# Delta rule steps in another order, and who makes the low weight parts of the second block

## The chip, the cores and the metric

The kernel runs on one core of one Trainium2 chip. The metric is the device time of one execution in microseconds (us). TensorE is PE in the profile, VectorE DVE, ScalarE ACT, GpSimd POOL and SyncE SP; SP issues the weight transfers.

## The reference

A sequence of 256 tokens with 1024 channels goes through a first block and then a second block, each of two layers. The change is in the second block, of which this is the mixer between two feed-forward networks, cut to what matters:

```python
hcat = x @ w_in
qa, ka, va, qkv_b, beta_raw, dt_raw, z, gate_raw = jnp.split(hcat, SPLIT_POINTS, axis=-1)
ya = sliding_window_attention(qa, ka, va, pos_bias, sink) @ w_branch_a      # 16 heads
qkv_b = jax.nn.silu(causal_depthwise_conv_2(qkv_b, conv_w))                 # 4 taps
qb, kb, vb = jnp.split(qkv_b, (QK_B, 2 * QK_B), axis=-1)                    # 8 heads of 128
qb, kb = l2norm(qb), l2norm(kb)
beta = jax.nn.sigmoid(beta_raw)
g = -jnp.exp(a_log) * jax.nn.softplus(dt_raw + dt_bias)
o = gated_delta_rule(qb, kb, vb, g, beta)
o = o * lax.rsqrt(jnp.mean(o * o, -1, keepdims=True) + NORM_EPS) * dn_norm_g * jax.nn.silu(z)
gate_a, gate_b = jnp.split(jax.nn.sigmoid(gate_raw), 2, axis=-1)
return (gate_a * ya + gate_b * (o @ w_branch_b)) @ w_out
```

The delta rule is, for each head, S_t = a_t (S_{t-1} - beta_t k_t k_t^T S_{t-1}) + beta_t k_t v_t^T and o_t = S_t^T q_t; the kernel computes it in two chunks of 128 tokens.

## The kernel before

**Weights in two parts.** All weights arrive as float32 in units of 128x2048, through a ring of four slots, issued by SP as slots come free. ACT makes the high part of each unit (L1506, called by split_high) and another engine the low part, weight minus high part (split_low: L1830 on DVE, L901 on GpSimd). PE multiplies three times: high by high, high by low, low by high. So one product round is three matmuls of 256 columns, and most units are 16 rounds, 48 matmuls. Which engine makes a low part is set by close(): GpSimd for the kinds named in by_pool, here "w" (projections) and "gy" (gates), except behind FFN units; DVE for the rest and for the whole first block. Splits are issued in quarters between the steps.

**A plan per block.** plan_second() writes one list of steps. Each engine walks that list in order and does its own part of every step, so the list fixes the order on PE, ACT, DVE and GpSimd at once; semaphores only add waits. A PSUM bank is passed on by two counters, full (PE has written it) and taken (ACT or DVE has read it).

**Weaving.** interleave(chain, dense) puts a chain of small dependent steps between rounds of big products. Each chain step has a weight; behind it as many rounds of the dense units follow as its share of the total weight. When a unit is complete, its follow-up steps come one at a time behind the next chain steps: for a convolution unit the taps of its two halves (DVE L2191, L2193, then tanh on ACT L1731) and silu (DVE L2206).

**The mixer.** First the attention: for head n score (PE L1212; DVE L2011 to L2018; exponentials on ACT L1617 to L1622), turn (transposes, PE L1227), value (PE L1256). cumg (PE L1356, DVE L2159 to L2166, two exponentials on ACT) makes the cumulative decays and stands ahead of score 0. Dense units in this weave are two queries, the convolutions of head pair 0, two z projections (pz) and the convolutions of pair 1.

Then the delta rule, two heads at a time. A head is prepared by five steps: dtr (PE transposes q, k and v, L1371; ACT squares L1745; GpSimd's root L858, L860), dte (six DVE scalars L2216 to L2221, then six scaled copies on DVE L2227 and five on ACT), ddc (PE L1397, DVE L2236, ACT L1776, GpSimd L949), dtf (PE L1383, L1387; DVE L2244), dkk (PE L1406; DVE L2252, L2257). ddc and dkk use bank 3, dtr and dtf banks 6 and 7 (4 and 5 for head 1). dtr waits for the silu of its pair; CO holds one pair's convolutions, so the first taps of the next wait for the second dtr of the pair.

solve() runs a pair a, b: dl0 (PE L1415, DVE L2265, L2267), then six levels of dla a, dla b, dlb a, dlb b. dla is two products (PE L1426) that ACT copies (L1506); dlb is four (PE L1436, L1438) with which DVE updates the inverse (L2274, L2279). Then du1 (L1447), du2 (L1454), du3 (L1460), evacuated by ACT, and du4 (L1468): ACT squares the output (L1796), GpSimd takes the root, DVE waits for the root and scales (L2287). dot transposes the result (PE L1477) and DVE multiplies and splits it (L2294, L1837, L1839). The preparation of the next two heads is inserted in the chain of a pair. Dense units: gate 0 and the convolutions of pair 2 in pair 0; gate 1 and the convolutions of pair 3 in pair 1; two pz and two gates in pair 2; four gates in pair 3. Behind the last pair come the gates of the second branch (gy, PE L1316 and L1322; DVE L2094, L2099) with the output product wo (L1080).

## Time and profile before

| what | us |
| --- | --- |
| median of three runs (lowest, highest) | 3360.16 (3359.53, 3362.44) |
| the profiled execution | 3359.86 |
| its span, first to last instruction | 3358.1 |
| PE busy in the span | 3068.3 |
| DVE busy | 1926.3 |
| ACT busy | 1340.5 |
| GpSimd busy | 526.1 |

Times inside the span count from its first instruction. The second block runs from about 1545 us; its first mixer from 1764 to 2232, its second from 2657 to 3130. Matmul ends are modelled by the profile, so the rate at which PE works is best read from the distance between starts. "idle before" names what ended an engine's idle time; a wait put down to "issue" was for nothing that the profile shows.

### The profile page before, as it was taken

Reading aid. Unit: us, or ns where it says so; the run is one execution under the profiler, and the core shown is the slowest. Engines: PE = TensorE matmul, PEld = TensorE weight load, DVE = VectorE, ACT = ScalarE, POOL = GpSimd, SP = SyncE. Lnnn points to the kernel's source line nnn. Section 1 sums busy time; section 2 is a strip of 40 time slices with the busy share of each in tenths; the row PEclk is TensorE's granted clock in tenths of the full one; section 3 lists DMA queues with packets and bytes.
Section 4 is the critical chain, followed back from the end, with each engine's and each line's share of the span. In section 5 each row is a group of like instructions: output and inputs, shape, how many; then the busy total and the mean of one; then the engine's idle time right before and its main releaser. Section 6 shows DMA issues by size and latency. Waiting matters only on the chain.

```text
span 3358.1 us, 59079 instructions
## 1 busy us (share of the span) xinstructions
PE 3068.3 (91%) x22178; PEld 2902.8 (86%) x22178; DVE 1926.3 (57%) x3302; ACT 1340.5 (40%) x2222; POOL 526.1 (16%) x469
## 2 busy tenths in 40 slices
PE   7999999998999999997998888989989898889897
PEld 7989898997989898996987888879979788789797
DVE  4556776554556776554553666375565536655654
ACT  3344454334344454332334544333333354343332
POOL 1000000000000000000004444430020235345101
PEclk9999999999999999998997999989989899999899
DMA  5544444554544445557552211345545422124453
GB/s 198 186 160 151 132 142 167 186 187 147 187 160 161 130 141 183 173 181 168 203 195 76 101 62 65 114 155 187 189 154 194 143 90 89 66 72 146 159 185 116
DMA packets 72121, 495.48 MB, mean 148 GB/s; under 512 B 8000, under 2 KB 8176, under 8 KB 19856
## 3 DMA queue, kind: packets, MB, share of 16 engines
q1 hardware_dynamic: 67504, 471.95, 41.2%
q0 software_dynamic: 4048, 18.59, 2.1%
q8 instruction: 184, 3.01, 0.4%
q14 instruction: 113, 0.93, 0.1%
q10 hardware_dynamic: 272, 0.99, 0.1%
HBM read 487.31 MB, written 4.19 MB: 146 GB/s over the span
## 4 chain that ended last, share of the span: by engine, by line
issue 75%; PE 11%; DVE 6%; POOL 4%; DVEq 1%; POOLq 1%; ACT 1%; DMA 0%; ACTq 0%; SPq 0%
PE psum L1102 4%; POOL weights_low L901 2%; DVE work L2193 1%; PE psum L1316 1%; POOL small L860 1%; PE psum L1322 1%; PE psum L1212 1%; POOLq L859 0%; DVE normed_t_low L1839 0%; DVE small L2218 0%; DVE work L2279 0%; PE psum L1158 0%; PE psum L1426 0%; DVEq L2196 0%; DVE normed_t_high L1837 0%
## 5 line engine op out<-in xcount | busy, mean ns | idle before, releaser
L1830 DVE TENSOR_TENSOR weights_low<-weight_ring,weights_high 128x2048 fp32r<-128x2048 f32 (+6 forms) x532 | 890.0, 1679 | 796.7 <-ACT weights_high L1506 795.5
L1506 ACT ACTIVATE weights_high<-weight_ring 128x2048 fp32r<-128x2048 f32 (+3 forms) x788 | 906.9, 1171 | 1099.1 <-DMA weight_ring<-stream 1091.1
L1027 PE MATMUL psum<-normed_t_high,weights_high 128*128 128x256 f32 x2816 | 803.5, 285 | 24.8 <-DVE normed_t_low L1839 22.3
L1027 PE MATMUL psum<-normed_t_low,weights_high 128*128 128x256 f32 x2816 | 800.8, 284 | 0.0
L1027 PE MATMUL psum<-normed_t_high,weights_low 128*128 128x256 f32 x2816 | 800.5, 284 | 0.0
L1027 PEld LDWEIGHTS psum<-normed_t_high,weights_high 128*128 128x128 f32 x2816 | 543.8, 193 | 31.5 <-DVE normed_t_low L1839 24.5
L1027 PEld LDWEIGHTS psum<-normed_t_low,weights_high 128*128 128x128 f32 x2816 | 544.6, 193 | 3.6
L1027 PEld LDWEIGHTS psum<-normed_t_high,weights_low 128*128 128x128 f32 x2816 | 544.3, 193 | 0.0
L1080 PE MATMUL psum<-weights_high,work_parts 128*128 128x512 f32 x1664 | 524.3, 396 | 13.9 <-DVE work_parts L1839 13.9
L1102 PE MATMUL psum<-normed_t_high,weights_high 128*128 128x256 f32 x1248 | 395.6, 317 | 11.5 <-DVE normed_t_low L1839 10.5
L901 POOL TENSOR_TENSOR weights_low<-weight_ring,weights_high 128x512 fp32r<-128x512 f32 (+1 forms) x216 | 348.4, 1628 | 307.4 <-ACT weights_high L1506 307.3
L1080 PEld LDWEIGHTS psum<-weights_high,work_parts 128*128 128x128 f32 x1664 | 306.2, 188 | 80.1 <-DVE work_parts L1839 14.4
L1102 PE MATMUL psum<-normed_t_low,weights_high 128*128 128x256 f32 x1248 | 362.2, 290 | 0.0
L1102 PE MATMUL psum<-normed_t_high,weights_low 128*128 128x256 f32 x1248 | 362.0, 290 | 0.0
L858 POOL TENSOR_TENSOR small<-small 128x1 f32<-128x1 f32 (+3 forms) x74 | 17.0, 230 | 2124.5 <-ACT work L1554 974.9
L1080 PE MATMUL psum<-weights_low,work_parts 128*128 128x512 f32 x832 | 328.5, 395 | 0.0
L1102 PEld LDWEIGHTS psum<-normed_t_high,weights_high 128*128 128x128 f32 x1248 | 249.0, 200 | 25.6 <-DVE normed_t_low L1839 11.9
L1102 PEld LDWEIGHTS psum<-normed_t_low,weights_high 128*128 128x128 f32 x1248 | 249.5, 200 | 1.0
L1316 PE MATMUL psum<-normed_t_high,weights_high 128*128 128x256 f32 x768 | 236.7, 308 | 14.8 <-DVE weights_low L1830 9.5
L1102 PEld LDWEIGHTS psum<-normed_t_high,weights_low 128*128 128x128 f32 x1248 | 248.0, 199 | 0.0
L1316 PE MATMUL psum<-normed_t_low,weights_high 128*128 128x256 f32 x768 | 222.7, 290 | 0.0
L1316 PE MATMUL psum<-normed_t_high,weights_low 128*128 128x256 f32 x768 | 222.5, 290 | 0.0
(258 smaller groups left out, 4326.8 us busy)
## 6 DMA issues: line engine op xcount, KB each, us to landing
weight_ring<-stream SPq DMA_DIRECT2D x400, 1024.0 KB, 4.9
weight_ring<-stream SPq DMA_DIRECT2D x64, 768.0 KB, 4.2
feature_rows<-feat POOLq DMA_DIRECT2D x6, 1024.0 KB, 5.0
work<-toeplitz_rows POOLq DMA_DIRECT2D x8, 512.0 KB, 6.6
feature_rows<-feat POOLq DMA_DIRECT2D x6, 512.0 KB, 4.0
toeplitz_rows<-work POOLq DMA_DIRECT2D x1, 3072.0 KB, 37.0
params<-prms POOLq DMA_DIRECT2D x5, 251.5 KB, 3.2
residual<-x SPq DMA_DIRECT2D x1, 1024.0 KB, 7.4
```

The lines of the kernel that those rows point to most:

```text
L858: pool.tensor_tensor(dst, src, EPSES[:, EPS_AT[eps], 0:n], ALU.add)
L860: pool.tensor_tensor(dst, dst, HALFNEG[:, 0:dst.shape[1]], ALU.pow).then_inc(signal, 1)
L901: pool.tensor_tensor(some(LOW, i, q, n), some(RING, i, q, n), some(HIGH, i, q, n).bitcast(F32), ALU.subtract).then_inc(low_by_pool, n)
L1027: ins = pe.matmul(PS[:, bank, at:at + S], w[a][:, first + k, c * P:(c + 1) * P], src[b][:, k, :], start=(k, m) == (0, 0), stop=(k, m) == ( ...
L1080: ins = pe.matmul(PS[:, b, :], src[c][:, r, t * P:(t + 1) * P], w[a][:, r, n * HALF:(n + 1) * HALF], start=start and m == 0, stop=stop and ...
L1102: ins = pe.matmul(PS[:, job.bank, c * S:(c + 1) * S], w[i][:, k, c * P:(c + 1) * P], XT[j][:, k, :], start=(k, m) == (0, 0), stop=(k, m) = ...
L1212: ins = pe.matmul(dst, q[:, t * P:(t + 1) * P], k[:, 0:keys], start=True, stop=not extra, skip_group_check=True)
L1316: ins = pe.matmul(PS[:, job.bank, 0:S], w[p][:, r, 0:P], XT[q][:, r, :], start=(r, m) == (0, 0), stop=(r, m) == (KB - 1, 2), skip_group_ch ...
L1322: ins = pe.matmul(PS[:, job.bank, S:2 * S], w[p][:, r - KB, P:2 * P], y[q][:, r - KB, :], start=(r, m) == (KB, 0), stop=(r, m) == (15, 2), ...
L1506: return act.activation(dst, src, ACT.Copy, scale=scale)
L1830: dve.tensor_tensor(some(LOW, i, q, n), some(RING, i, q, n), some(HIGH, i, q, n).bitcast(F32), ALU.subtract).then_inc(low_by_vector, n)
L2193: last = dve.scalar_tensor_tensor(out=co[:, n:S], in0=src, scalar=tap, in1=co[:, n:S], op0=ALU.mult, op1=ALU.add)
```

## The change

The steps and their arithmetic stay the same; their order in the list, one bank use and the maker of low parts are other. In plan_second():

- by_pool is empty: DVE makes every low part of the second block.
- cumg moves from ahead of the attention to the tenth place of its chain.
- Two heads are prepared together: dtr, dte, dtr, dte, then ddc, dtf, ddc, dtf, then both dkk (before: all steps of a head, then the next, and for heads 0 and 1 a mixed order). In the chain of a pair the first eight come at every fourth place from the third, the two dkk behind both du4.
- The scaling of the output leaves DVE's part of du4 and becomes a step of its own, dsc, behind both du4.
- The first gate unit is woven into the attention. In pairs 0 and 1 the three convolutions come first and one other unit last; pair 2 has one pz and three gates, pair 3 three gates.

```diff
@@ -354,7 +354,7 @@
 
 
 def plan_second():
-    pl = Plan(("w", "gy"))
+    pl = Plan()
     acc_lo = [(b, 1, 1) for b in range(4)]
     acc_hi = [(b, 1, 1) for b in range(4, 8)]
     def begin(s):
@@ -401,8 +401,6 @@
     for p in range(2):
         pl.steps.append(query(p)[0])
     pl.step("pv", "pv", banks=["lo"], unit=("w", 5))
-    pl.step("cumg", "cumg", banks=["s"],
-            signals=[("decay_diff_ready", 1), ("decay_exps_ready", 1), ("decay_scalars_ready", 1)])
     def attention():
         steps = []
 
@@ -446,24 +444,30 @@
         return pl.make("gy", ("gy", i * KB + k), j=i * KB + k, banks=[bank], i=i, k=k, unit=("gy", i, k),
                        signals=[("gate_tanh_ready", 1)] + last), []
 
-    def prepare(h, banks):
-
-        a, b, c = banks
-        return [lambda: pl.step("dtr", ("dtr", h), banks=[a, b], h=h,
-                                signals=[("qk_squares_summed", 1), ("qk_rsqrt_ready", 1)]),
-                lambda: pl.step("dte", ("dte", h), h=h, signals=[("head_scalars_ready", 1)]),
-                lambda: pl.step("ddc", ("ddc", h), banks=[c], h=h,
-                                signals=[("decay_ready", 1), ("strict_decay_ready", 1)]),
-                lambda: pl.step("dtf", ("dtf", h), banks=[a, b], h=h),
-                lambda: pl.step("dkk", ("dkk", h), banks=[c], h=h, signals=[("level_masked", 1)])]
+    def prepare(hs, banks):
+
+        steps = []
+
+        def add(h, kind, banks, signals=()):
+            steps.append(lambda: pl.step(kind, (kind, h), banks=banks, h=h, signals=signals))
+
+        for h, b in zip(hs, banks):
+            add(h, "dtr", b, [("qk_squares_summed", 1), ("qk_rsqrt_ready", 1)])
+            add(h, "dte", [], [("head_scalars_ready", 1)])
+        for h, b in zip(hs, banks):
+            add(h, "ddc", [3], [("decay_ready", 1), ("strict_decay_ready", 1)])
+            add(h, "dtf", b)
+        for h in hs:
+            add(h, "dkk", [3], [("level_masked", 1)])
+        return steps
 
     def solve(hs):
 
         steps = []
 
-        def both(kind, signals=(), banks=1, **a):
+        def both(kind, signals=(), **a):
             for h in hs:
-                steps.append(lambda h=h: pl.step(kind, (kind, h) + tuple(a.values()), banks=[4 + h % 2] * banks,
+                steps.append(lambda h=h: pl.step(kind, (kind, h) + tuple(a.values()), banks=[4 + h % 2],
                                                  h=h, signals=signals, **a))
 
         both("dl0")
@@ -474,28 +478,36 @@
         both("du2")
         both("du3")
         both("du4", [("out_squares_summed", 1), ("out_rsqrt_ready", 1)])
+        for h in hs:
+            steps.append(lambda h=h: pl.step("dsc", ("dsc", h), h=h))
         both("dot", [("delta_out_ready", 1)])
         return steps
 
     steps, last = attention()
-    first = [prepare(0, (6, 7, 3)), prepare(1, (4, 5, 3))]
-    chain = steps + [(4, first[0][0])] + last + [(4, f) for f in first[0][1:2] + first[1][:1] + first[0][2:4]
-                                               + first[1][1:2] + first[0][4:] + first[1][2:]]
+    steps.insert(9, (2, lambda: pl.step("cumg", "cumg", banks=["s"],
+                                        signals=[("decay_diff_ready", 1), ("decay_exps_ready", 1),
+                                                 ("decay_scalars_ready", 1)])))
+    first = [(4, f) for f in prepare((0, 1), ((6, 7), (4, 5)))]
+    chain = steps + first[:1] + last + first[1:]
     dense = [(16, lambda p=p: query(p)) for p in (2, 3)] + [(16, lambda w=w: conv(0, w)) for w in range(3)]
     dense += [(16, lambda p=p: gated(p)) for p in range(2)] + [(16, lambda w=w: conv(1, w)) for w in range(3)]
+    dense += [(16, lambda: gate(0, 0, "lo3"))]
     interleave(pl, chain, dense)
 
     pairs = NH_B // 2
-    extra = [[(16, lambda: gate(0, 0, "lo3"))] + [(16, lambda w=w: conv(2, w)) for w in range(3)],
-             [(16, lambda: gate(0, 1, "lo3"))] + [(16, lambda w=w: conv(3, w)) for w in range(3)],
-             [(16, lambda p=p: gated(p)) for p in (2, 3)] + [(16, lambda k=k: gate(0, k, "lo3")) for k in (2, 3)],
-             [(16, lambda k=k: gate(0, k, "lo3")) for k in range(4, 8)]]
+    extra = [[(16, lambda w=w: conv(2, w)) for w in range(3)] + [(16, lambda: gate(0, 1, "lo3"))],
+             [(16, lambda w=w: conv(3, w)) for w in range(3)] + [(16, lambda: gated(2))],
+             [(16, lambda: gated(3))] + [(16, lambda k=k: gate(0, k, "lo3")) for k in range(2, 5)],
+             [(16, lambda k=k: gate(0, k, "lo3")) for k in range(5, 8)]]
     for hp in range(pairs):
         chain = [(2, f) for f in solve((2 * hp, 2 * hp + 1))]
         if hp + 1 < pairs:
-            todo = [f for h in (2 * hp + 2, 2 * hp + 3) for f in prepare(h, (6, 7, 3))]
-            for n, f in enumerate(todo):
-                chain.insert(2 + 3 * n, (2, f))
+            todo = [(2, f) for f in prepare((2 * hp + 2, 2 * hp + 3), ((6, 7), (6, 7)))]
+            ends = chain[-4:]
+            chain = chain[:-4]
+            for n, item in enumerate(todo[:8]):
+                chain.insert(2 + 4 * n, item)
+            chain += todo[8:] + ends
         interleave(pl, chain, extra[hp])
     pl.step("feature", signals=[("feature_rows_loaded", 16)], s=1)
     for k in range(2):
@@ -2280,9 +2292,10 @@
                                                masks[:, st.s - 1, o:o + 1, :].to_broadcast([P, T, P]), new)
                 last.then_inc(bank_taken[job.bank], 1)
 
-            def du4(st):
-                job, i = st.jobs[0], st.h % 2
-                dve.wait_ge(out_rsqrt_ready, reach("out_rsqrt_ready", st.at["out_rsqrt_ready"]))
+            def dsc(st):
+                done, i = named(("du4", st.h)), st.h % 2
+                job = done.jobs[0]
+                dve.wait_ge(out_rsqrt_ready, reach("out_rsqrt_ready", done.at["out_rsqrt_ready"]))
                 for t in range(T):
                     last = dve.tensor_scalar(OD[:, i, t, :], PS[:, job.bank, t * P:(t + 1) * P],
                                              RSO[:, 2 * i + t:2 * i + t + 1], None, ALU.mult)
@@ -2310,7 +2323,7 @@
             walk(dve, {"xt": xt, "gu": gu, "score": score, "out_norm": out_norm, "gy": gy, "factors": factors,
                        "small_split": small_split,
                        "post2": post2, "ps": ps, "cumg": cumg, "pz": pz, "taps": taps, "silu": silu, "dte": dte, "ddc": ddc,
-                       "dtf": dtf, "dkk": dkk, "dl0": dl0, "dlb": dlb, "du4": du4, "dot": dot,
+                       "dtf": dtf, "dkk": dkk, "dl0": dl0, "dlb": dlb, "dsc": dsc, "dot": dot,
                        "out_turn": out_turn}, 2, low=split_low)
 
 
```

## Rows read from the trace of the kernel before

**Rows 1.** The page: span, and busy time of each engine.
```profile
span 3358.1 us, 59079 instructions
PE 3068.3 (91%) x22178; PEld 2902.8 (86%) x22178; DVE 1926.3 (57%) x3302; ACT 1340.5 (40%) x2222; POOL 526.1 (16%) x469
```
**Rows 2.** PE's waits, 1760 to 2200 us: us in total, times, longest.
```profile
PE psum L1371 <- DVE work L2206: 15.4, 3, 5.2
...
PE psum L1426 <- DVE work L2279: 5.2, 5, 1.6
PE psum L1227 <- ACT work L1619: 4.5, 1, 4.5
PE psum L1477 <- DVE work L2287: 4.4, 8, 1.1
```
**Rows 3.** Pairs 0 to 3: length, busy PE, PEld, DVE, ACT, POOL; clock, DMA.
```profile
1923.50:1988.40 64.90, 53.03 (x413) 50.57 (x412) 42.55 (x118) 26.09 (x81) 28.97 (x30) 0.95 0.19 66
1988.40:2053.20 64.80, 52.77 (x412) 50.42 (x411) 40.80 (x119) 25.28 (x79) 26.05 (x29) 0.95 0.19 66
2053.20:2114.20 61.00, 52.38 (x413) 50.42 (x412) 34.64 (x103) 25.58 (x77) 26.07 (x29) 0.94 0.21 70
2114.20:2161.00 46.80, 43.33 (x372) 42.52 (x371) 16.66 (x56) 17.36 (x46) 21.70 (x21) 1.00 0.26 91
```
**Rows 4.** PE in order of time, a dtr at half rate and one at full.
```profile
1931.25 1.54 PE L1371 MATMUL psum<-constants,work 128*128 128x128 f32 x6 [5.21 <-DVE work L2206]
...
1950.94 0.82 PE L1371 MATMUL psum<-constants,work 128*128 128x128 f32 x6
```
**Rows 5.** PE in order of time: three other long gaps.
```profile
1819.25 0.90 PE L1227 MATMUL psum<-constants,work 128*128 128x128 f32 x3 [4.53 <-ACT work L1619]
...
1914.81 0.75 PE L1397 MATMUL psum<-work,constants 128*128 128x256 f32 x2 [2.65 <-DVE work L2252]
...
2164.14 0.38 PE L1316 MATMUL psum<-normed_t_high,weights_high 128*128 128x256 f32 x1 [2.65 <-DVE work L2094]
```
**Rows 6.** DVE and GpSimd in order of time: the same kinds, held and not.
```profile
1811.90 4.34 DVE L2164 TENSOR_TENSOR small<-small 128x16 f32<-128x16 f32 x1
...
2172.75 4.23 DVE L2099 TENSOR_TENSOR work<-work 128x256 f32<-128x256 f32 x1
...
2181.72 0.42 DVE L2099 TENSOR_TENSOR work<-work 128x256 f32<-128x256 f32 x1
...
1780.48 5.57 POOL L901 TENSOR_TENSOR weights_low<-weight_ring,weights_high 128x2048 fp32r<-128x2048 f32 x1 [6.27 <-ACT weights_high L1506]
```
**Rows 7.** DVE and PE in order of time: dte, taps, the root of du4.
```profile
1956.22 1.25 DVE L2218 TENSOR_TENSOR small<-small 128x2 f32<-128x2 f32 x1
...
1957.58 0.20 DVE L2221 TENSOR_SCALAR small<-small 128x1 f32<-128x1 f32 x1
...
1959.95 0.48 DVE L2191 TENSOR_SCALAR work<-psum,params 128x256 f32<-128x256 f32 x1
1960.50 1.59 DVE L2193 SCALAR_TENSOR_TENSOR work<-psum,params,work 128x255 f32<-128x255 f32 x3
...
1959.54 0.71 PE L1436 MATMUL psum<-work 128*128 128x128 f32 x4 [1.12 <-ACT work L1506]
...
1985.68 0.61 DVE L2287 TENSOR_SCALAR work<-psum,small 128x128 f32<-128x128 f32 x2 [4.88 <-POOL small L860]
```
**Rows 8.** Groups by line and shape: GpSimd from 1500, DVE up to 1530 us.
```profile
L901 POOL TENSOR_TENSOR weights_low<-weight_ring,weights_high 128x512 fp32r<-128x512 f32 x192 | 244.8, 1292 | 206.0 <-ACT weights_high L1506 205.9
L901 POOL TENSOR_TENSOR weights_low<-weight_ring,weights_high 128x2048 fp32r<-128x2048 f32 x20 | 94.1, 4704 | 88.7 <-ACT weights_high L1506 88.7
...
L1830 DVE TENSOR_TENSOR weights_low<-weight_ring,weights_high 128x2048 fp32r<-128x2048 f32 x166 | 379.8, 2292 | 407.0 <-ACT weights_high L1506 407.0
...
L1830 DVE TENSOR_TENSOR weights_low<-weight_ring,weights_high 128x512 fp32r<-128x512 f32 x60 | 40.3, 686 | 2.3 <-ACT weights_high L1506 2.3
```
**Rows 9.** ACT in order of time, ahead of score 0.
```profile
1809.62 1.91 ACT L1506 ACTIVATE weights_high<-weight_ring 128x2048 fp32r<-128x2048 f32 x1 [2.87 <-DMA weight_ring<-stream]
```

## Prediction

> **What bounds the kernel now.** I began with the busy times [rows 1]: PE works for 3068 of 3358 us, DVE for 1926. PE is the bound, so only idle PE time and time at the lower TensorE clock can be won. The change touches the mixer of the second block alone, in two layers; the first block and all FFN stretches keep their instructions. Next I read who PE waits for in the first layer's mixer [rows 2]: the longest entry is the transposes of a new head (dtr, L1371), which wait three times for DVE's silu of the convolution, 5.1 us each. The second layer's list has the same rows in the same sizes. Then the four pairs of heads as stretches [rows 3]: 64.9, 64.8, 61.0 and 46.8 us, with PE busy for 53.0, 52.8, 52.4 and 43.3. Last the queues around single waits, in order of time [rows 4 to 9].
>
> Three readings carry the sum. First, a long wait costs more than itself. After the 5.21 us gap before dtr the matmuls come 0.21 us apart instead of 0.12, and six transposes take 1.54 instead of 0.82 us [rows 4]: half rate, 1.2 instead of 2.4 GHz. Against the same instructions at full rate that loses 0.7 + 6 x 0.09 + 0.6 + 3 x 0.09 = 2.1 us, so a dtr costs 7.3 us. The same follows the 4.53 us gap in the attention, until 1826.5 (about 3.2 us lost) and gaps of only 2.65 us (L1397 takes 0.75 instead of 0.59, then 16 matmuls stand 0.09 too far apart: 1.6 us) [rows 5], but not the 1.1 to 1.6 us waits [rows 2]. Second, GpSimd's low parts delay DVE: L2099 takes 4.23 us once and 0.42 the next time, L2218 1.25 instead of 0.15, L2164 4.34 [rows 6]. Third, DVE and ACT are in-order queues that carry everything: the taps of half a convolution are 0.48 + 1.59 us, the work for one head (dte) 2.5 us without such stalls, and PE's dlb at 1959.54 starts 1.9 us after DVE's last scalar, because ACT's copy for it stands behind ACT's five dte copies [rows 7].
>
> **The change part by part**, per layer. Pure PE time is the busy time of a stretch less its half-rate loss: 53.0 - 2.1 = 50.9 us in pair 0.
>
> *Low parts to DVE.* 192 quarters, 4 halves and 20 whole units go from GpSimd to DVE [rows 8], 35 units a layer. A quarter (128x512) costs DVE 0.69 us where it does this already, a whole unit 2.29; GpSimd's are 1.29 and 4.70 us. A pair gets 16 quarters, 11 us. Against that stand stalls that end: in pair 0 L2218 and L2216 (3.7 us), L2267 (1.9), L2257 and L1839 (1.8), together 7.4. DVE's useful work in pair 0 goes from 42.5 - 7.4 = 35.1 to 46 us, of some 60. In the gate units after the delta rule the stall of L2099 is larger than the new 2.29 us, and a unit gives PE 5.8 us (48 x 0.12), so there it is hidden. No PE wait on a low part by GpSimd stands in the lists, so the move itself wins nothing there.
>
> *Start of the attention.* cumg leaves the place before score 0. Its L2164 is held for 4.34 us by GpSimd's whole unit, and turn 0 waits 4.53 us for that [rows 5, 6]. What is late next is the low part of the unit whose high part ACT ends at 1811.5 (it waits for DMA until 1809.6) [rows 9]: on DVE it now stands ahead of score 0, until 1813.8. Score 0 and the exponentials take 2.3 us more, to 1816.2; PE, without cumg's 1 us, arrives at 1813.7. A wait of 2.6 us and 1.6 of half rate stay, of 4.5 and 3.2: -3.4. Taps and a split together now stand before some scores whose slack is about 2 us: +0.5 (from 0 to 3). The gate unit moved here adds its 5.8.
>
> *Preparing heads 0 and 1.* Before, from the first dtr (1895.17) to dtr of head 2 (1931.25) is 36.1 us, plus 2.1 at half rate. The bank clash in which ddc of head 1 waits for dkk of head 0 (2.65 us) goes. But now all three convolutions of pair 1 and some 11 quarters stand in DVE's queue before dtr of head 2: 19.5 us of work as now, 4.9 for the last convolution, 7 for the quarters. Worse, the squares of head 1 on ACT now stand behind the second tanh, which stands behind DVE's taps, which stand behind dte of head 0. Walked through: dte 0 on DVE at 8.1 to 10.6 us after the first dtr, taps to 12.7, squares to 15.5, GpSimd's root to 17, dte 1 to 19.5. ddc 1 waits 4 us for bank 3, dkk 0 and dkk 1 some 2 each, and dtr of head 2 starts at 38 us with its silu just done. With two half-rate stretches (3.1) and less the 1.4 us of gate work already counted: 39.7 against 38.2, so +1.5.
>
> *Pairs 0 and 1.* The 7.3 us of dtr go: the silu is there long before. The other waits of pair 0 are 6.7 us now. In the new order I walked the queues step by step: (i) dte of the first head stands between the two dlb updates, which with a quarter makes dla of the second head wait 1.7; (ii) the order taps, quarter, taps, dte, silu of the second head makes dlb wait 1.7 and 2.7, the second with 1.7 of half rate; (iii) the second convolution's taps, ddc and silu stand before an update: 1.8; (iv) the third convolution's tanh stands before the evacuations of du2 and du3: 2.6; (v) dkk and dot 1.2. Sum 11.7 + 1.7 = 13.4, so a pair takes 50.9 + 13.4 = 64.3. Pair 0, without its dtr, was 57.6: +6.7. Pair 1 was 64.8: -0.5.
>
> *dsc.* DVE sat 4.88 us in du4 for the root [rows 7]; that was idle time. Setting the scaling apart gives PE two more portions of dense work (1 us) before dot, so the waits of dot, 0.74 and 0.23 per pair, nearly go; they are in (v). It costs no instruction.
>
> *Pair 2* has no convolution in the new order: waits 1.7 + 0.9 + 1.8 for dte, a second dte, and gate and dot steps: 52.4 - 2.1 + 4.4 = 54.7 against 61.0, so -6.3. *Pair 3* gives up one unit: 43.3 - 5.8 + 2 of waits = 39.5 against 46.8, so -7.3. Three units for 38 steps still give 0.45 us between steps, enough for ACT's and DVE's answers of 0.6 and 1.0 us around the other head's step. *After it* the first gate waits 2.65 us and loses 1.6 [rows 5], partly because GpSimd holds L1839 for 0.9; without that I expect 1.3 and no fall: -3.
>
> Sum per layer: -3.4 + 0.5 + 5.8 + 1.5 + 6.7 - 0.5 - 6.3 - 7.3 - 3.0 = -6.0, for two layers -12.0. The profiled execution took 3359.9 us (span 3358.1), 0.3 below the median of the runs. Forecast: **3348 us**.
>
> **The rivals.** *The cover works* (3313 us): steps that I let collide slip past each other, since a PE that waits once gives DVE time for the next. If the waits in pairs 0 and 1 are half of 13.4 and the preparation wins 4, a layer wins 17.4 more. For it: DVE still has 14 of 60 us free. Against it: the collisions are fixed by the order of in-order queues.
>
> *Slower* (3373 us): DVE becomes the bound where convolutions, dte and quarters meet. If two more waits per pair are long enough to drop the clock (2 x 1.7 in two pairs), the preparation loses 3 more and the attention's start wins nothing (2.9), a layer is 12.7 us worse than forecast, 6.7 slower than before. It decides from the point where waits and half rate of pairs 0 and 1 pass 16.4 us each. For it: DVE is busy for 42.6 of 64.9 us in pair 0 already [rows 3] and gets 11 more. Against: a PE that waits lets DVE catch up, and pairs 2 and 3 have no convolutions.
>
> *No change* (3358 us): the stall turns round. DVE's splits read two SBUF operands as GpSimd's did, and GpSimd's whole unit took 5.57 us once, 4.70 in the mean [rows 6, 8]. Then GpSimd's roots for dtr and du4 (1.01 us) are held for up to a quarter, 0.65 us, 16 times a layer; if half of that is on the path, 5.2 us cancel the gain. By the Trainium skill, SBUF — State Buffer, section "SBUF: two separate sides", whichever of a VectorE op with two SBUF inputs and a GpSimd op comes first holds the shared ports for its whole length; by that rule the loss goes both ways, and this rival would hold.
>
> **How the numbers follow.** Forecast 0.36, the cover works 0.24, no change 0.18, slower 0.22. A measurement of this kernel tells about 0.2%, 6.7 us, from no change. The forecast's own spread (3338 to 3358) puts a fifth of it within 0.2%, but a part of the no-change case falls below: faster 0.55, same 0.22, slower 0.23. The range reaches from beyond the better case, 3305, to beyond the worse, 3378; all waits gone would be near 3240, and I leave that out.
>
> **What would show it.** L1371 should no longer wait for L2206 in pairs 1 and 2; L2099 should be 0.42 us everywhere; L1436 should wait longer for ACT and L1397 for DVE before pair 0. Pairs should be near 64, 64, 55 and 40 us. I am wrong if pairs 0 and 1 come out under 60 (DVE's queue had more slack than I gave it) or over 68.

## The result and the profile after

The changed kernel takes 3367.9 us in the median (3363.7 to 3380.8), the kernel before 3360.8 on the same chip: a ratio of 1.0023, 95% interval 1.0016 to 1.003. It is slower by 7.1 us, where I forecast 3348 us and a gain of 12. The time lies inside the range given (3305 to 3378).

The page of the changed kernel, against [rows 1]: GpSimd's work went from 526 to 182 us, DVE's rose by 63, and PE, the bound, is "busy" 13 us longer with the same instructions, because more of them ran at the lower clock.

```profile
span 3367.2 us, 59075 instructions
PE 3081.4 (92%) x22178; PEld 2914.3 (87%) x22178; DVE 1989.2 (59%) x3516; ACT 1340.7 (40%) x2222; POOL 182.3 (5%) x253
```

The first layer's mixer by stretches: the attention (first score to first dtr), the preparation of heads 0 and 1 (first dtr to first dl0), then pairs 0 to 3. Columns are length, busy PE, PEld, DVE, ACT and POOL, granted clock, DMA.

```profile
1810.80:1902.10 91.30, 85.14 (x595) 76.17 (x594) 52.25 (x167) 47.57 (x140) 0.00 (x0) 0.93 0.27 93
1902.10:1943.30 41.20, 29.02 (x205) 27.91 (x206) 28.83 (x74) 17.17 (x49) 4.19 (x8) 0.88 0.22 77
1943.30:2008.00 64.70, 53.69 (x413) 51.52 (x411) 45.82 (x134) 26.08 (x80) 6.79 (x12) 0.95 0.20 66
2008.00:2072.90 64.90, 53.95 (x413) 51.58 (x411) 45.47 (x135) 25.45 (x79) 6.20 (x12) 0.95 0.19 66
2072.90:2125.90 53.00, 49.96 (x413) 48.36 (x411) 34.03 (x111) 24.88 (x76) 6.46 (x12) 1.00 0.24 81
2125.90:2165.80 39.90, 37.87 (x319) 36.45 (x317) 20.98 (x66) 14.87 (x41) 1.78 (x4) 1.00 0.23 80
```

Against [rows 3] the pairs read 64.7, 64.9, 53.0 and 39.9 us, where 64, 64, 55 and 40 had been forecast. The same two stretches ahead of them in the kernel before:

```profile
1811.10:1895.20 84.10, 76.99 (x551) 68.54 (x551) 40.47 (x139) 44.76 (x136) 33.60 (x24) 0.94 0.26 88
1895.20:1923.50 28.30, 25.65 (x194) 25.12 (x195) 22.64 (x57) 15.81 (x47) 17.11 (x18) 0.94 0.34 113
```

So the loss stands ahead of the pairs: the attention is 7.2 us longer and the preparation 12.9, of which the pairs give back 14 to 15. PE's waits from 1760 to 2200 us (total, times, longest), against [rows 2]:

```profile
PE psum L1448 <- ACT work L1518: 8.6, 5, 2.8
PE psum L1438 <- DVE work L2291: 7.9, 6, 2.1
...
PE psum L1409 <- DVE work L2248: 6.6, 1, 6.6
...
PE psum L1418 <- DVE work L2264: 4.8, 4, 3.5
...
PE psum L1114 <- DVE weights_low L1842: 2.0, 1, 2.0
```

The transposes' wait of 15.4 us for the silu is gone, as forecast. In its place stand ddc of head 1 (L1409, one wait of 6.64), dkk (L1418), and shorter waits in the pairs. (Lines of the engine code are 12 higher than before: dtr is now L1383, ddc L1409, dkk L1418, dlb L1448.)

In what follows, "lost to half rate", or "half rate" with a number, is what a stretch lost by it: the sum of one minus the granted clock over windows of 1 us. That sum also counts time in which PE was idle anyway, so it can't simply be added to a wait that it overlaps; "half rate while PE works" leaves the idle time out. The times of the experiments are medians, and the ratio is against the kernel before on the same chip.

### The profile page after: what moved, and what is told of

The parts are those of the page before. It is cut to its first block, busy times and chain, and to the rows that moved or that the text cites. A ratio compares the mean times of both kernels' runs of the same rounds, so it can differ in the third digit from the quotient of the medians.

```text
span 3367.2 us, 59075 instructions
## 1 busy us (share of the span) xinstructions
PE 3081.4 (92%) x22178; PEld 2914.3 (87%) x22178; DVE 1989.2 (59%) x3516; ACT 1340.7 (40%) x2222; POOL 182.3 (5%) x253
## 4 chain that ended last, share of the span: by engine, by line
issue 86%; DVE 5%; PE 4%; POOL 2%; DVEq 2%; POOLq 1%; ACT 1%; ACTq 0%
DVE work L2205 1%; POOL small L872 1%; PE psum L1114 1%; DVE weights_low L1842 1%; POOLq L935 1%; POOL residual L936 1%; DVEq L2208 1%; DVEq L2284 0%; POOLq L871 0%; DVE work L2203 0%; PE psum L1418 0%; PE psum L1334 0%; PE psum L1450 0%; PE psum L1438 0%; DVE normed_t_low L1851 0%
## 5 line engine op out<-in xcount | busy, mean ns | idle before, releaser
L1842 DVE TENSOR_TENSOR weights_low<-weight_ring,weights_high 128x2048 fp32r<-128x2048 f32 (+4 forms) x746 | 1070.7, 1441 | 884.1 <-ACT weights_high L1518 881.6
L1328 PE MATMUL psum<-normed_t_high,weights_high 128*128 128x256 f32 x768 | 236.8, 308 | 14.1 <-DVE weights_low L1842 9.4
L1092 PEld LDWEIGHTS psum<-weights_low,work_parts 128*128 128x128 f32 x832 | 156.6, 188 | 38.2
L1518 ACT ACTIVATE work<-psum 128x256 f32<-128x256 f32 (+4 forms) x276 | 117.5, 431 | 157.1 <-PE psum L1438 69.7
```

Source lines behind the costliest of these rows:

```text
L1092: ins = pe.matmul(PS[:, b, :], src[c][:, r, t * P:(t + 1) * P], w[a][:, r, n * HALF:(n + 1) * HALF], start=start and m == 0, stop=stop and ...
L1328: ins = pe.matmul(PS[:, job.bank, 0:S], w[p][:, r, 0:P], XT[q][:, r, :], start=(r, m) == (0, 0), stop=(r, m) == (KB - 1, 2), skip_group_ch ...
L1518: return act.activation(dst, src, ACT.Copy, scale=scale)
L1842: dve.tensor_tensor(some(LOW, i, q, n), some(RING, i, q, n), some(HIGH, i, q, n).bitcast(F32), ALU.subtract).then_inc(low_by_vector, n)
```

## Experiments: which part costs

**The low parts alone.** The old order, with all low parts of the second block on DVE.

```diff
-    pl = Plan(("w", "gy"))
+    pl = Plan()
```

> The kernel before with one edit: by_pool is empty, so DVE makes all low parts, in the old order of steps. Theory A (DVE's queue costs where steps already crowd it): the three waits of dtr per layer stay, GpSimd's holds on DVE go, turn 0 waits 2 us less; the preparation of heads 0 and 1 gets some 7 us of quarters less 5 us of stalls; in all 0 to +3 us a layer, 3360 to 3366. Rival B (the low parts on DVE are what costs, the order wins): +6 to +10 us a layer, 3372 to 3380. If it is faster than before by 5 us or more, the loss sits in the order alone.

Measured: 3365.2 us, ratio 1.0012 (1.0003 to 1.0022), 3.9 us slower. That is inside theory A's range and under rival B's. The attention is 89.2 us long with an unchanged order (84.1 before), the preparation 32.4 (28.3).

**The order alone.** The changed kernel with its low parts given back to GpSimd.

```diff
-    pl = Plan()
+    pl = Plan(("w", "gy"))
```

> The changed kernel with GpSimd making the low parts as before: the new order alone. Theory A: from first dtr to first dl0 the stretch is 34 to 38 us (28.3 before, 41.2 with the change), because the order itself makes dte of head 1 late; pairs 2 and 3 keep their gain; about -3 to -6 us a layer, 3348 to 3354. Rival B: the preparation is back near 30 us, -10 us a layer or more, under 3341. Theory C (the order is all of the loss): 3364 or more.

Measured: 3358.1 us, ratio 0.9992 (0.9982 to 1.0001), 3.1 us faster by the medians, not more than can be measured. Theory A had the preparation right (35.0 us, 34 to 38 expected) and the time 4 us too low. So the low parts cost 3.9 us in the old order and 9.8 in the new one (3367.9 - 3358.1): the two halves of the change hinder each other. At the start of the attention this kernel shows why moving cumg gained little by itself. DVE, GpSimd and PE in order of time (start, duration):

```profile
1813.28 4.53 DVE L2030 TENSOR_SCALAR small<-small 128x2 f32<-128x2 f32 x1
...
1813.27 4.51 POOL L913 TENSOR_TENSOR weights_low<-weight_ring,weights_high 128x2048 fp32r<-128x2048 f32 x1 [1.07 <-ACT weights_high L1518]
...
1818.95 0.68 PE L1239 MATMUL psum<-constants,work 128*128 128x128 f32 x2 [3.94 <-ACT work L1631]
```

Before, GpSimd's whole unit held cumg's L2164 for 4.34 us [rows 6]. With cumg gone it holds the next DVE operation that works in SBUF alone, one of the first score (0.23 us otherwise), and PE waits 3.94 us instead of 4.53, with the same 5.1 us of half rate behind it.

**The scaling step alone**, added to the kernel before.

```diff
+        for h in hs:
+            steps.append(lambda h=h: pl.step("dsc", ("dsc", h), h=h))
...
-            def du4(st):
-                job, i = st.jobs[0], st.h % 2
-                dve.wait_ge(out_rsqrt_ready, reach("out_rsqrt_ready", st.at["out_rsqrt_ready"]))
+            def dsc(st):
+                done, i = named(("du4", st.h)), st.h % 2
+                job = done.jobs[0]
+                dve.wait_ge(out_rsqrt_ready, reach("out_rsqrt_ready", done.at["out_rsqrt_ready"]))
```

> The kernel before with the scaling of the output as a step of its own behind both du4, nothing else. Theory A: the waits of dot (0.74 and 0.23 us a pair) become 0.5 at most, and DVE's idle time in du4 turns into room: -0.5 us a pair, 3356 to 3359. Rival: the other waits of the pair take it up, 3360.

Measured: 3363.4 us, ratio 1.0002 (0.9992 to 1.0011). No gain, as the rival had it. Dot's waits keep their sum over the four pairs (4.4 us, in 3 waits instead of 8) and a wait of dkk for ACT's copy, 4.0 us in two, is new.

**The scaling step taken out** of the changed kernel, the reverse edit.

```diff
-        for h in hs:
-            steps.append(lambda h=h: pl.step("dsc", ("dsc", h), h=h))
...
-            ends = chain[-4:]
-            chain = chain[:-4]
+            ends = chain[-2:]
+            chain = chain[:-2]
```

> The changed kernel with the output scaling back in du4 (no dsc step). My forecast gave the step about 1 us per pair (dot waits 0.74 and 0.23 before). In the kernel before, adding the step alone changed the time by less than can be measured. Theory 'dsc counts for nothing': time within 3 us of the changed kernel's. Rival 'it helps in the new order, where dkk stands before it': without it DVE sits in du4 waiting for GpSimd's root up to 4.9 us with ddc and the quarters behind it, pairs get 2 to 3 us longer each, and the time goes up by 8 or more.

Measured: 3371.7 us, ratio 1.0033 (1.0021 to 1.0045), 3.8 us more than the changed kernel by the medians: between the two expectations, with intervals that overlap. The rows side with the rival in kind, not in size. The four pairs take 226.5 us instead of 222.5 (226.6 instead of 225.3 in the second layer), and dkk, which waits 0.43 us in each of these pairs in the changed kernel, waits 2.1, since DVE sits in du4 with dkk's masking behind it; over both layers PE waits 9 us more without the step (98.2 against 89.2). PE's waits in the pairs without the step:

```profile
PE psum L1416 <- DVE work L2262: 6.3, 3, 2.1
```

## Experiments: why the preparation is long

**The old order of the preparation**, in the changed kernel.

```diff
-    chain = steps + first[:1] + last + first[1:]
+    chain = steps + first[:1] + last + [first[n] for n in (1, 2, 4, 5, 3, 8, 6, 7, 9)]
```

> The changed kernel with the steps that prepare heads 0 and 1 in their old order behind the attention (dtr 0, out_turn, dte 0, dtr 1, ddc 0, dtf 0, dte 1, dkk 0, ddc 1, dtf 1, dkk 1), all else new. Theory A: the 6.6 us wait of ddc 1 for ddc 0 goes, since DVE's ddc 0 no longer stands behind dte 1; ddc 1 waits for dkk 0 instead, 3 to 4 us; the stretch from the first dtr to the first dl0 is 37 to 39 instead of 41.2: -2 to -4 us a layer, 3360 to 3364. Rival B (only the amount of work in DVE's queue counts): the same 41 us, 3368.

Measured: 3371.9 us, ratio 1.0037 (1.0024 to 1.005). Theory A had the stretch right (39.0 us from first dtr to first dl0, 37 to 39 expected), and here ddc of head 1 waits 4.8 us for the bank of dkk (L2264). But the time missed both expectations: the pairs take 228.1 us instead of 222.5. Their waits are the same (11.1 and 11.0 us in pairs 0 and 1, against 11.0 and 11.0); what grew is half rate, 6.8 us in each instead of 3.4. Pairs 0 and 1 of this kernel:

```profile
1938.80:2006.10 67.30, 56.20 (x413) 53.86 (x412) 45.92 (x135) 26.24 (x81) 6.65 (x12) 0.90 0.19 64
2006.10:2074.00 67.90, 56.95 (x413) 54.45 (x411) 45.48 (x135) 25.56 (x79) 6.19 (x12) 0.90 0.18 63
```

The old order is not the cure. Why the clock fell more often behind it, no run shows.

**dtr of head 1 earlier.** The chain of the 6.64 us wait, in order of time on ACT, GpSimd, DVE and PE of the changed kernel:

```profile
1918.36 0.42 ACT L1743 ACTIVATE work<-work 128x256 f32<-128x256 f32 x1 [2.40 <-DVE work L2205]
...
1919.20 0.26 ACT L1757 ACTIVATE work<-psum 128x128 f32<-128x128 f32 x1
...
1921.28 1.01 POOL L872 TENSOR_TENSOR small<-small 128x4 f32<-128x4 f32 x1
...
1922.32 0.17 DVE L2228 TENSOR_SCALAR small<-small 128x2 f32<-128x2 f32 x1 [1.90 <-POOL small L872]
...
1925.80 0.34 DVE L2248 SCALAR_TENSOR_TENSOR work<-psum,small,constants 128x128 f32<-128x128 f32 x1
...
1926.45 1.22 PE L1409 MATMUL psum<-work,constants 128*128 128x256 f32 x2 [6.64 <-DVE work L2248]
```

ACT's tanh (L1743) waits for DVE's taps; the squares of head 1 (L1757) are next in ACT's queue though their data has lain in PSUM since 1909.5; then comes GpSimd's root, DVE's dte of head 1, two quarters, and only then the decay of head 0 (L2248), whose bank PE wants. The edit puts the squares ahead of that tanh:

```diff
-    chain = steps + first[:1] + last + first[1:]
+    chain = steps + first[:1] + last + [first[n] for n in (2, 1, 3, 4, 5, 6, 7, 8, 9)]
```

> The changed kernel with one step moved: the transposes (dtr) of head 1 come before the work for head 0 (dte), so that the squares of head 1 on ACT stand ahead of the second tanh of the convolution. In the changed kernel the first matmul of ddc of head 1 waits 6.64 us in layer 1, because in DVE's queue ddc of head 0 stands behind dte of head 1, which waits for GpSimd's root, which waits for ACT's squares at 1919.20, which stand behind the tanh at 1918.36, which waits for DVE's taps. Theory 'order of the queues': the wait of 6.64 us falls to under 2, the stretch from the first dtr to dl0 goes from 41.2 to 35 or 36, and the time from 3368 to 3354 to 3361. Theory 'amount of work': DVE has 28.8 us of work in 41.2 us there and is itself the limit; then the wait only moves to dkk or dl0, the stretch stays at 39 or more, and the time within 4 us of the changed kernel's.

Measured: 3360.6 us, ratio 0.9998 (0.9989 to 1.0007): 7.3 us won, the whole loss of the change. ddc's wait falls from 6.64 to 1.37 us, the preparation from 41.2 to 37.9, the pairs stay (222.4). PE's waits in the preparation:

```profile
PE psum L1418 <- DVE work L2264: 3.5, 1, 3.5
PE psum L1395 <- DVE feature_rows L2239: 2.1, 1, 2.1
PE psum L1409 <- DVE work L2248: 1.4, 1, 1.4
```

The order of the queues was the cause of the long wait. The edit moves two things at once: the squares of head 1 now start at 9.6 us after the first dtr instead of 17.1, and the first taps, which wait for the same transposes (below), at 6.1 instead of 7.4. The stretch did not reach the 35 or 36 us that this theory gave, since dtf (L1395) now waits 2.1 us for dte of head 0, which came to stand behind the second half's taps.

**GpSimd for the low parts ahead of the pairs.** The changed kernel, with ten units given back.

```diff
-            self.by.append("pool" if key[0] in self.by_pool and not after_ffn else "vector")
+            self.by.append("pool" if i in self.by_pool and not after_ffn else "vector")
...
-    pl = Plan()
+    pl = Plan(range(40, 50))
```

> The changed kernel, but GpSimd makes the low parts of ten units (stream numbers 40 to 49, those due from the attention's start to the end of the preparation of heads 0 and 1); VectorE makes all others, as in the change. Theory 'splits hurt where convolutions stand': attention and preparation become those of the new order with GpSimd's parts (89.5 and 35.0 us against 91.3 and 41.2), the pairs stay as in the changed kernel (222.5 us), so a layer wins 8 and the time is 3350 to 3355. Theory 'it comes back later': the preparation is shorter but the pairs wait more, as when the old order of the preparation was tried; time 3361 to 3368.

**And with both edits:**

> The two edits together: dtr of head 1 before dte of head 0, and GpSimd's low parts for units 40 to 49. If the wait of ddc of head 1 comes from the order of the queues and the splits only add to it, the preparation goes to 32 or 33 us and the time to 3345 to 3352, below both kernels. If both edits remove the same wait, the time is that of the better of the two alone, within 3 us.

Measured: 3359.5 us (ratio 0.9997, 0.9988 to 1.0006) and 3362.6 us (0.9998, 0.9987 to 1.0008). Attention and preparation went where the first theory said: 88.6 and 35.0 us, and with both edits 88.4 and 31.9. But the times missed the ranges (3350 to 3355, and 3345 to 3352): pair 0 of the first layer grew from 64.7 to 74 us in both kernels, 3.7 us of it in waits and some 5.8 in half rate while PE works. Neither theory had this place. With both edits, PE's waits from 1931 to 1965 and what DVE and GpSimd did then:

```profile
PE psum L1427 <- DVE work L2269: 2.7, 1, 2.7
PE psum L1383 <- DVE work L2218: 1.7, 1, 1.7
```
```profile
1933.58 1.61 DVE L2269 TENSOR_TENSOR work<-work,constants 128x128 f32<-128x128 f32 x2
1935.11 2.84 DVE L2218 SCALAR_TENSOR_TENSOR work<-work 128x512 f32<-128x512 f32 x1
...
1933.57 3.83 POOL L913 TENSOR_TENSOR weights_low<-weight_ring,weights_high 128x512 fp32r<-128x512 f32 x2 [1.96 <-ACT weights_high L1518]
```

The pair of L2269 takes 0.49 us when DVE is alone, L2218 0.68 in the mean (8.2 us for 12). Here they take 1.61 and 2.84, and L2218 is the silu that dtr of head 2 needs.

**GpSimd for the attention alone**, and the early dtr. As the kernel with both edits, with fewer units:

```diff
-    pl = Plan(range(40, 50))
+    pl = Plan(range(40, 47))
```

> The changed kernel with dtr of head 1 before dte of head 0, and GpSimd's low parts for the seven units 40 to 46 alone (the attention), not for 47 to 49 (the preparation). With 40 to 49 on GpSimd pair 0 took 73.9 us against 64.7, and its rows show DVE held by GpSimd: L2269 1.58 and 1.61 us, L2218 2.84, with PE waiting 2.73 us in dl0 and 1.70 in dtr. Theory 'GpSimd's hold': pair 0 comes back to 65 or 66 us while the attention keeps 88.5, and the preparation takes 37 to 38 (as with the early dtr alone); time 3352 to 3357. Theory 'a shorter preparation is paid back in pair 0 whoever splits, since dtr of head 2 waits for the convolutions': preparation and pair 0 together stay at 105 or 106 us as with 40 to 49, and the time at 3359 to 3363.

Measured: 3351.2 us, ratio 0.9971 (0.996 to 0.9982), 9.7 us faster than the kernel before and faster than both kernels of the case. The two waits in dl0 and dtr are gone; PE's waits from 1931 to 1965:

```profile
PE psum L1448 <- ACT work L1518: 3.9, 2, 2.4
PE psum L1438 <- DVE work L2291: 1.2, 1, 1.2
PE psum L1438 <- DVE work L2279: 0.7, 1, 0.7
```

The preparation takes 36.7 us and pair 0 some 67.6 in the first layer, 37.5 and 65.6 in the second: 103 to 104 us together, against 105.8 with both edits and 105.9 in the changed kernel. GpSimd's hold on DVE in pair 0 was there, but taking it away won next to nothing in waits: preparation and pair 0 together wait for 20.7 us, against 19.9 with both edits, 19.7 with the early dtr alone and 24.4 in the changed kernel (first layer). What pair 0 no longer waits, the preparation does, as the second theory had it in kind. The rest is the clock: the attention fell from 88.4 to 86.4 us though it waits 2.64 and 1.47 us where the kernel with both edits waits 2.09 and 1.47 (below).

**The new order with GpSimd's parts, and the early dtr.** As the order alone, with the same permutation of the preparation.

> The new order with all its low parts on GpSimd (3358 us as measured), and dtr of head 1 before dte of head 0. Theory 'order of the queues': the early transposes win what they won with DVE's parts, 7 us, so 3350 to 3353. Theory 'GpSimd's hold takes it': root and taps wait for GpSimd's parts there, the stretch from the first dtr to dtr of head 2 stays at 40 us or more, and the time is 3356 to 3360.

Measured: 3352.2 us, ratio 0.9973 (0.9963 to 0.9984), 5.9 us below the order alone, and preparation 31.9 us instead of 35.0, 38.3 from the first dtr to dtr of head 2. The first theory holds. With this order, DVE's low parts cost 8.4 us (3360.6 - 3352.2).

**Another bank for dkk of head 1**, in the kernel with GpSimd for the attention.

```diff
-            add(h, "dkk", [3], [("level_masked", 1)])
+            add(h, "dkk", [5 if h == 1 else 3], [("level_masked", 1)])
```

> As the kernel with GpSimd's parts for units 40 to 46 and the early dtr, and dkk of head 1 writes to PSUM bank 5 instead of sharing bank 3 with dkk of head 0. With the early dtr alone its wait for DVE's L2264 was 3.51 us. Theory 'bank clash': the wait goes and the preparation is 3 us shorter, time 3 to 6 us below the kernel without this edit. Theory 'DVE's queue': L2264 of head 1 comes no earlier, since convolutions' taps stand ahead of it; PE waits 2 to 3 us in dl0 or dtr of head 2 instead, and the time stays within 3 us.

Measured: 3348.4 us, ratio 0.9957 (0.9944 to 0.9971), 2.8 us below the kernel without this edit, with intervals that overlap. The preparation is 33.0 us, pair 0 71.6: 104.6 together, no less than without. dkk's wait of 3.6 us went, and dl0 waits for the same DVE work instead:

```profile
PE psum L1427 <- DVE work L2269: 3.4, 2, 3.1
```

That is the theory "DVE's queue". It is the fastest kernel measured, but I can't claim that the edit is what made it so.

The stretches of the first layer, and the sum of attention, preparation and pairs over both layers, in us:

| kernel | attention | preparation | dtr 0 to dtr of head 2 | four pairs | sum, two layers | time against before |
|---|---|---|---|---|---|---|
| before | 84.1 | 28.3 | 36.1 | 236.8 | 701.7 | |
| changed | 91.3 | 41.2 | 42.8 | 222.5 | 712.7 | +7.1 |
| low parts alone | 89.2 | 32.4 | 39.9 | 233.5 | 709.6 | +3.9 |
| order alone | 89.5 | 35.0 | 41.4 | 227.1 | 702.4 | -3.1 |
| scaling step alone | 83.5 | 31.1 | 38.9 | 241.8 | 707.8 | +2.2 |
| old preparation | 91.4 | 39.0 | 40.6 | 228.1 | 716.2 | +10.7 |
| no scaling step | 91.6 | 41.3 | 42.9 | 226.5 | 718.8 | +11.2 |
| dtr 1 early | 91.4 | 37.9 | 39.5 | 222.4 | 706.0 | 0.0 |
| GpSimd for 40 to 49 | 88.6 | 35.0 | 41.5 | 233.2 | 707.9 | -1.0 |
| both | 88.4 | 31.9 | 38.3 | 233.0 | 706.9 | +2.0 |
| GpSimd for 40 to 46, dtr 1 early | 86.4 | 36.7 | 38.3 | 225.0 | 695.5 | -9.7 |
| order alone, dtr 1 early | 89.3 | 31.9 | 38.3 | 227.0 | 696.0 | -8.7 |
| dkk on bank 5 | 86.6 | 33.0 | 38.8 | 228.7 | 695.4 | -12.4 |

The sums come from one execution each, and no difference smaller than some 4 us in them is read. Against before they run 3 to 7 us above the times, since the stretches outside (ahead of the first score, and after the pairs) and the execution chosen are not in them.

**Waits or clock.** The same stretches of both layers, taken apart into PE's waits (as the view of waits counts them) and half rate while PE works, in us. What is left, the work at full rate, is 580 to 588 in every kernel.

| kernel | PE's waits | half rate while PE works |
|---|---|---|
| before | 92.6 | 26.6 |
| changed | 89.2 | 37.4 |
| low parts alone | 87.3 | 42.7 |
| order alone | 85.2 | 33.1 |
| scaling step alone | 96.6 | 29.4 |
| old preparation | 86.4 | 43.1 |
| no scaling step | 98.2 | 34.6 |
| dtr 1 early | 83.5 | 35.4 |
| GpSimd for 40 to 49 | 82.6 | 39.4 |
| both | 78.7 | 41.7 |
| GpSimd for 40 to 46, dtr 1 early | 79.1 | 29.1 |
| order alone, dtr 1 early | 82.8 | 28.5 |
| dkk on bank 5 | 79.2 | 28.2 |

The changed kernel does not wait longer than the one before: it waits 3.4 us less, and loses 10.8 us more at half rate while PE works. Before, a good part of the low clock fell into long waits, where it costs nothing. Inside the wait of 5.21 us for dtr, and behind two short waits of the changed kernel (1.06 and 1.07 us):

```profile
1929.00:1931.20 2.20, 0.00 (x0) 0.00 (x0) 1.27 (x4) 1.14 (x3) 0.07 (x1) 0.50 0.01 4
...
1997.90:2001.20 3.30, 3.30 (x18) 3.30 (x17) 0.69 (x2) 1.26 (x8) 0.89 (x2) 0.50 0.02 5
```

Half rate in all, idle time included, grew only from 37.5 to 41.0 us; the part of it inside waits fell from 10.9 to 3.6. No run held the clock fixed: that the change costs by way of the clock is read from these sums, one execution each, and not shown by an edit.

## Why the prediction was wrong, step by step

Forecast and measured, per layer, in the first layer:

| term | forecast | measured |
|---|---|---|
| attention, with its share of the gate unit and without cumg's old place | +1.5 | +6.4 |
| preparation, with its share of the gate unit | +2.9 | +5.6 |
| pair 0, as counted in the prediction | +6.7 | +7.1 |
| pair 1 | -0.5 | 0.0 |
| pair 2 | -6.3 | -8.0 |
| pair 3 | -7.3 | -6.3 |
| after the delta rule | -3.0 | +0.9 |
| sum | -6.0 | +5.7 |

(Attention: forecast -3.4 + 0.5 + 5.8 - 1.4; measured 91.3 - 84.1, less 0.8 by which the stretch ahead of it is shorter without cumg. Preparation: 41.2 + 64.7 for it and pair 0, less 28.3 + 64.9, is 12.7, of which 7.1 is pair 0's 64.7 - 57.6.)

*The pairs were right* in mechanism, and in their sum partly by luck: 222.5 us against 222.8 forecast, with pairs 0, 1 and 3 longer by 0.4, 0.6 and 0.4 us and pair 2 shorter by 1.7. The single waits of pair 0 came as walked (1.7, 1.7, 2.7, 1.8, 2.6 and 1.2 forecast; 1.20, 1.50, 2.42, 2.05, 2.13 and 0.91 measured). dtr no longer waits for the silu, dlb waits longer for ACT (8.6 against 3.4 us), and DVE is busy for 45.8 us in pair 0 where 46 was worked out. Three other terms were off, by 4.9, 2.7 and 3.9 us, and they make up 11.5 of the 11.7 us between the sums. In the second layer the whole mixer is 4.2 us longer, with the same pattern.

*Start of the attention: the wait was right, the clock was not.* The wait fell from 4.53 to 2.15 us (2.6 forecast). Half rate while PE works fell from 3.7 to 3.4, where 3.2 to 1.6 had been forecast, so the place gives 2.6 us and not 3.4. Neither half of the change gives it alone: with cumg's move alone the wait is 3.94 us, with the low parts alone it is 1.62 and 0.76 in two waits, and in both kernels half rate stays at 5.1 us, idle time included.

*"Taps and a split together now stand before some scores whose slack is about 2 us: +0.5": this step failed.* It was given 0 to 3 us and costs about 5. DVE has 0.7 us of a quarter, two times 2.1 us of taps and 1.7 us of the values' scaling to do ahead of one score; PE waits 1.03 us, then 1.79, and the clock falls. PE in order of time, and the window behind it (clock in the third column from the end):

```profile
1864.89 0.41 PE L1268 MATMUL psum<-work 128*128 128x64 f32 x2 [1.03 <-DVE work L2085]
...
1868.30 1.65 PE L1224 MATMUL psum<-work 64*128 64x128 f32 x4 [1.79 <-DVE small L2030]
```
```profile
1868.00:1870.00 2.00, 1.70 (x5) 1.05 (x5) 1.42 (x3) 1.72 (x7) 0.00 (x0) 0.53 0.02 4
```

Waits 2.8 and half rate 3.4 us, less a wait of 1.4 for ACT near the same place in the kernel before, which is gone: 4.8. With the start (-2.6) and the gate unit (5.8 less 1.4) that makes 6.6, where 6.4 us were measured. The low parts alone, in the old order, wait 1.7 us for DVE's L2018 at the same place and lose 5.1 us to half rate from 1871; before, nothing. With the order alone the wait there is 0.64 us and the clock stays. So it is the low parts on DVE that cost here. I looked at each wait as a price of its own and took waits of 1.1 to 1.6 us as free of half rate; here, and behind 1.06 and 1.07 us in pair 0, waits of that size were followed by it.

*The preparation: the queue was named rightly and timed wrongly.* The walk had the squares of head 1 behind the second tanh, but dte of head 0 done at 10.6 us after the first dtr and dte of head 1 at 19.5. They were done at 14.1 and 22.5. The taps ahead of dte 0 wait for the transposes of head 1, which still read the convolution buffer; they end 7.4 us after the first dtr:

```profile
1909.54 0.48 DVE L2203 TENSOR_SCALAR work<-psum,params 128x256 f32<-128x256 f32 x1 [2.42 <-PE psum L1383]
...
1912.78 1.23 DVE L1842 TENSOR_TENSOR weights_low<-weight_ring,weights_high 128x1024 fp32r<-128x1024 f32 x1 [1.07 <-ACT weights_high L1518]
```

A half unit of low parts (1.23 us, and 1.07 for its high part) stands between them and dte 0. The walk named waits of 8 us (4 at ddc, 2 at each dkk); measured are 12.2: 2.05 for that low part, which the walk did not have, 6.64 at ddc, and 3.50 at one dkk, with none at the other. Half rate while PE works is 3.3 us, 3.1 forecast. From the first dtr to dtr of head 2 that makes 42.8 us where the forecast's figures give 41.1 (38 and 3.1). The other 1.0 of the 2.7 us is an error of counting: the preparation was taken up to dtr of head 2 and pair 0 from the first dl0, so the stretch between them counts twice, 2.5 us of work before and 1.6 after. That the place of dtr of head 1 is behind the long wait is shown by the early dtr, which wins 7.3 us with DVE's low parts and 5.9 with GpSimd's.

*After the delta rule: failed.* The gain of 3 rested on GpSimd's hold of 0.9 us going away. It went, but a quarter of low parts came to stand in the same place of DVE's queue, and PE waits 2.34 us (2.65 before). Nor did the clock hold, as forecast: half rate while PE works is 3.0 us behind this wait, 1.7 before, so the place costs 1 us more. DVE, then PE:

```profile
2165.66 0.68 DVE L1842 TENSOR_TENSOR weights_low<-weight_ring,weights_high 128x512 fp32r<-128x512 f32 x1
2166.26 0.47 DVE L2307 SCALAR_TENSOR_TENSOR work<-psum,small,work 128x256 f32<-128x256 f32 x1
...
2169.28 0.58 PE L1328 MATMUL psum<-normed_t_high,weights_high 128*128 128x256 f32 x1 [2.34 <-DVE work L2106]
```

*The rivals.* The result is nearest to "slower" (3373 us), whose mechanism, DVE as the bound where convolutions, dte and quarters meet and waits long enough to drop the clock, is the one that acted. It acted elsewhere: the point that I gave for it, 16.4 us of waits and half rate in pairs 0 and 1, was not reached (11.0 and some 3.4 us each). "The cover works" is excluded by the same rows. "No change" had the stall turned round, DVE's splits on GpSimd's roots. It exists: L870 takes 0.20 us, but 1.06, 0.46 and 0.72 when a split is under way, and L872 kept its 1.01. That is 1.6 us in a layer, and no wait in PE's list is put down to it. One such place, DVE and GpSimd:

```profile
2077.64 0.68 DVE L1842 TENSOR_TENSOR weights_low<-weight_ring,weights_high 128x512 fp32r<-128x512 f32 x1
...
2077.66 0.72 POOL L870 TENSOR_TENSOR small<-small 128x4 f32<-128x4 f32 x1 [10.19 <-ACT work L1757]
```

Both end at 2078.3 to 2078.4. By this, the trace agrees with the rule cited from the Trainium skill (SBUF — State Buffer, section "SBUF: two separate sides") in both directions. That this rival had no weight here fits the short splits of DVE (0.7 us); no run tested it.

*What stays open.* It is not known why the clock falls behind one short wait and not behind another. The 11 us between the kernel with both edits and the one with GpSimd for units 40 to 46 are not waits (78.7 and 79.1 us) but half rate (41.7 and 29.1). That is not the luck of the traced execution alone: the seven executions of the latter have a mean granted clock of 0.954 or 0.955, while the eleven of the former run from 3347.9 us at 0.956 to 3365.0 at 0.949. Whether GpSimd's parts or the mere timing of the waits does it, the runs don't separate.

## What to carry to other kernels

Moving work off an engine that was never waited for, onto one whose in-order queue feeds the bound, can cost even where that engine is idle for 40% of the time: 3.9 us here in the old order, 9.8 in the new. A sum of waits does not show it: PE waited less in both kernels with DVE's low parts than before, but more of its work ran at half rate. When a step is moved, look for the operation that is ready and stands behind one that isn't (here squares with their data in PSUM for 10 us, behind a tanh that waits for another engine); putting it first won 7.3 and 5.9 us. And price a reordering where it puts things as well as where it takes them from: the first layer's pairs came out in sum as forecast, and the loss stood ahead of them, with 1 us behind, where the moved work and the low parts went.

## What the runs showed of the chip that I had not expected

The same wait does not always cost the same. Ahead of the same score, two kernels that differ only in three later units of low parts wait 1.47 us for DVE. In the kernel with GpSimd for units 40 to 49 and the early dtr the clock then drops; with 40 to 46 it does not. Three windows of each from the wait on:

```profile
1867.00:1869.00 2.00, 1.81 (x10) 1.34 (x10) 1.39 (x7) 1.83 (x7) 0.06 (x1) 0.93 0.02 4
1869.00:1871.00 2.00, 1.87 (x9) 1.71 (x9) 1.16 (x3) 1.49 (x5) 2.00 (x2) 0.50 0.00 0
1871.00:1873.00 2.00, 2.00 (x15) 2.00 (x14) 1.34 (x3) 1.85 (x6) 1.41 (x2) 0.72 0.35 49
```
```profile
1864.00:1866.00 2.00, 1.79 (x10) 1.25 (x10) 1.32 (x7) 2.00 (x8) 0.28 (x1) 1.00 0.01 4
1866.00:1868.00 2.00, 1.94 (x17) 1.94 (x18) 1.58 (x3) 1.47 (x7) 2.00 (x2) 1.00 0.00 0
1868.00:1870.00 2.00, 2.00 (x19) 2.00 (x19) 1.36 (x3) 2.00 (x7) 1.41 (x2) 1.00 0.75 160
```

At the attention's start a wait of 2.64 us lost 1.7 us to half rate in one kernel, 2.15 us lost 3.4 in another, and 4.53 lost 5.1. In the pairs of the changed kernel a wait of 2.05 us at 1984.7 kept full rate, while 1.06 and 1.07 us, two microseconds apart at 1995 and 1997, lost 1.7. Even one kernel differs from layer to layer: pair 0 of the changed kernel takes 64.7 us in the first layer and 67.5 in the second, with 11.0 us of waits in both, the same to 0.1 us line by line. The second layer's row:

```profile
2841.70:2909.20 67.50, 56.52 (x412) 54.24 (x411) 45.72 (x133) 26.19 (x80) 6.75 (x12) 0.90 0.19 64
```

So a stretch of a single execution can't be trusted to better than 2 or 3 us where a wait ends near it, and differences of that size in the tables above are not explained by the edits alone.
